# The late halves of the modulation are spread to all partitions by two fp32r passes instead of one f32 matmul

## The chip, the cores and the metric

The kernel runs on one core of a Trainium2 chip. The metric is the device time of one launch in microseconds. Its five engines work side by side and are tied only by semaphores: TensorE (PE), VectorE (DVE), ScalarE (ACT), GpSimd (POOL), and SyncE (SP), which here issues nearly all loads.

## The reference, cut to what matters

One transformer block: a norm scaled and shifted by a modulation, a mixer of three kinds of attention, and a feed-forward part that chooses experts by product keys (PEER). x is 512 tokens by 1024. The part at issue is the modulation: `c` is one vector of 1024, and its product with `w_ada` gives 6144 numbers, six rows of 1024, which are the same for each token.

```python
cs = jax.nn.silu(c)
mod = jnp.einsum('bd,de->be', cs, w_ada[l]) + b_ada[l]
sh1, sc1, g1, sh2, sc2, g2 = [m[:, None, :] for m in jnp.split(mod, N_MOD, axis=-1)]
h = rmsnorm(x, norm1_g[l]) * (1.0 + sc1) + sh1
x = x + g1 * mixer(h, w_in[l], w_out[l], lam, lam_init, subln_g[l], sinks[l])
h = rmsnorm(x, norm2_g[l]) * (1.0 + sc2) + sh2
x = x + g2 * peer_ffn(h, peer_wq[l], peer_keys[l], peer_u[l], peer_v[l])
```

## The kernel before

**The modulation.** Six rows are cut into twelve halves of 512 columns, numbered 0 to 11 in the order sc1, sh1, g1, sc2, sh2, g2 (`ADA_HALVES`). A half's weights, 1024 x 512, lie in SBUF as eight blocks of 128 x 512, one of the 1024 inputs to a partition and block. VectorE multiplies each block by its column of silu(c) and adds them up (`mod_half`, L1588; eight instructions at L1599 and L1602), which leaves 128 partial sums for each column in `mod_acc`. The sum over the partitions is TensorE's: a matmul with a 128 x 128 matrix of ones as weights (`mod_row`, L516; the matmul at L521) adds them up and writes the total to all 128 partitions of a bank of PSUM, "a row". VectorE then copies the row to its place in SBUF (`mod_row` of VectorE, L1609: L1615 or L1618). Halves 0 to 3 (sc1, sh1) are needed as columns and go another way; halves 4 to 11 are the eight late ones.

**The precision.** An f32 matmul takes the engine longer than one of the rounded format fp32r (the rows below show both). Large products in this kernel are made in fp32r: an operand is split into a rounded part (hi) and the rest (lo), and two or three fast passes are added up in PSUM. The weights of ones need no split.

**The order around it.** Each engine's program is written out by hand. The mixer runs 64 jobs, J = 0 to 63 (a tile of 128 tokens and a head; the heads of one kind have two softmax maps each): TensorE makes the scores (L611) two jobs ahead; VectorE scales and masks them (L1707, the softmax step); ScalarE takes the exponential (L1311); for that kind VectorE combines the two maps (L1723 to L1727, `combine`); TensorE transposes the result (L624) and multiplies it with the values (L644). Between them TensorE makes projections of x with w_in (L562 to L564 and L582 to L584), whose weights ScalarE rounds (L1263) and GpSimd subtracts (L1167), with loads by SyncE (L1012). The late halves are threaded through this. Half 4 is summed on VectorE before the jobs (L1676, L1679), half 5 right behind it (L1689), and their rows come between the first projections. Of halves 6 to 11 two of the eight blocks are added in each of four jobs out of five: half 6 + J//5, its last two in J = 3, 8, 13, 18, 23, 28 (L1836). The row of a half is asked for by TensorE in J = 5, 10, ... 30 (L734), behind that job's part of a projection, and copied out by VectorE in the same J (L1838), behind the softmax step, a combine if there is one, and the first two sums of the next half.

**What ties them.** `s_accd` counts summed halves. TensorE waits for it before a row; SyncE waits for it before it loads the weights of the half after next into the same place (L1002), and its other loads stand behind that in its queue. Rows and projections take turns in two banks of PSUM (G and S2), each of which must be copied out before it is filled again. The scores take turns in S0 and S1, which the softmax step frees. `done(engine, instruction, semaphore)` makes an engine wait for its own result before it goes on.

Of the kernel before, what the change touches and what calls it, by code (L numbers as in the profile page):

```python
# [6 lines left out]
P = 128  # L7
D, S = 1024, 512
KD = D // P
# [88 lines left out]
def peer_block_kernel(nc, x, c_col, norm1_col, w_ada, b_ada, w_in, w_out, lam_vecs, subln_row, sinks_row,  # L98
# [4 lines left out]
    with ctx:  # L103
        def sb(name, shape, dt=f32):
            return ctx.enter_context(nc.sbuf_tensor(name, shape, dt))

        def sem(name):
            return ctx.enter_context(nc.semaphore(name))
# [4 lines left out]
        def at(name, kib, shape, dt=f32):  # L113
            return nc.alloc_sbuf_tensor_at(name, shape, dt, offset=base + int(kib * 1024))
# [22 lines left out]
        g1_row = at("g1_row", 168, [P, D])  # L137
        g2_row = at("g2_row", 172, [P, D])
        mod_acc = at("mod_acc", 176, [P, 2, 512])
        sh_acc = at("sh_acc", 184, [P, D])  # L140
        o_tile = [at(f"o_tile{i}", kib, [P, D]) for i, kib in enumerate((140, 144, 180, 184))]
        o_sq = at("o_sq", 188, [P, NA * HD])
# [59 lines left out]
        fin_row = at("fin_row", 96, [P, D])  # L202
        ident = sb("ident", [P, P])
        ones = sb("ones", [P, P])
        dist = sb("dist", [P, S])
        dist_w = sb("dist_w", [P, 2 * P])
        q_scale = sb("q_scale", [P, len(Q_TILES)])
# [55 lines left out]
        s_inhi, s_inlo = sem("w_in_hi_ready"), sem("w_in_lo_ready")  # L263
        s_h1hi, s_h1lo = sem("h1_hi_ready"), sem("h1_lo_ready")
        s_wout_c = sem("w_out_of_c_loaded")
        s_wohi, s_wolo, s_othi = sem("w_out_hi_ready"), sem("w_out_lo_ready"), sem("o_hi_ready")
        s_wout, s_keys, s_fin = sem("w_out_loaded"), sem("keys_loaded"), sem("final_loaded")
        s_wq = [sem(f"wq_loaded{j}") for j in range(4)]
# [120 lines left out]
        ADA_HALVES = [(s, b) for s in ADA_ORDER for b in range(2)]  # L389

        ADA_PIECES = [(0, 0, 2), (0, 2, 4), (0, 4, 6), (0, 6, 8), (1, 0, 2), (1, 2, 4), (1, 4, 6), (1, 6, 7), (1, 7, 8)]
        XT_BANKS = ["S2", "S0", "S1", "T0", "T1", "O0", "O1", "S2"]

        def key_tiles(i, j):
# [61 lines left out]
        def _(pe):  # L456
# [59 lines left out]
            def mod_row(n):  # L516

                b = side["next"]
                ps = take(b, ("row", n))
                pe.wait_ge(s_accd, n + 1)  # L520
                pe.matmul(ps[:, :], ones[:, :], mod_acc[:, n % 2, :], start=True, stop=True).then_inc(full[b], 1)  # L521

            def first_two():

# [617 lines left out]
        def _(pool):  # L1142
# [2 lines left out]
            pool.memset(power[:, :], -0.5).then_inc(s_power, 1)  # L1145
            pool.memset(ident[:, :], 0.0).then_inc(s_const, 1)
            pool.memset(ones[:, :], 1.0).then_inc(s_const, 1)
            pool.iota(dist[:, :], [[-1, S]], base=S - P, channel_multiplier=1,
                      allow_small_or_imprecise_dtypes=True).then_inc(s_const, 1)
            pool.iota(iota16[:, :], [[1, TOPK]], base=0, channel_multiplier=0,  # L1150
# [419 lines left out]
        def _(dve):  # L1570
# [17 lines left out]
            def mod_half(n, first, last):  # L1588

                acc = mod_acc[:, n % 2, :]  # L1590
                w = ada_late[n % 2]
                if first == 0:
                    half_used(dve, n - 2)
                    dve.wait_ge(s_ada[n % 2], 16 * ((n - 4) // 2 + 2))
                for k in range(first, last):
                    if k == 0:

                        dve.wait_ge(s_bh[n % 3], 16 * ((n - 4) // 3 + 1))
                        ins = dve.scalar_tensor_tensor(out=acc, in0=w[:, k, :], scalar=c_silu[:, k:k + 1],  # L1599
                                                       in1=b_half[:, n % 3, :], op0=ALU.mult, op1=ALU.add)  # L1600
                    else:
                        ins = dve.scalar_tensor_tensor(out=acc, in0=w[:, k, :], scalar=c_silu[:, k:k + 1], in1=acc,  # L1602
                                                       op0=ALU.mult, op1=ALU.add)
                    if k < KD - 1:
                        done(dve, ins, s_dv)
                    else:
                        ins.then_inc(s_accd, 1)

            def mod_row(n):  # L1609
                ps = taken(dve, ("row", n))  # L1610
# [621 lines left out]
```

## Time and profile before

| | |
|---|---|
| median of 3 runs | 1568.89 us (1568.38 to 1573.02) |
| profiled execution | 1570.63 us |
| its span in the trace | 1568.8 us |
| TensorE busy | 1526.6 us (97%) |
| VectorE busy | 1338.7 us (85%) |
| ScalarE, GpSimd busy | 660.1 us (42%), 486.0 us (31%) |
| spread matmuls (L521) | first at 69.5 us, last at 170.5 us |
| mixer with its projections | to some 310 us; behind it the experts |

A busy share of TensorE says little by itself, since its matmuls overlap and their ends are modelled; the distance of two starts is the time that one takes of the engine. In a timeline a bracket behind an instruction gives how long its engine stood idle before it, and which instruction ended that. Idle time of an engine counts only where another waits for it.

### The profile page before, as it was taken

To read this page: it belongs to the slowest core of one execution; us is meant where nothing else is said; L and a number is where in the kernel's file an instruction comes from. 1 tells how busy PE (TensorE), PEld (TensorE's weight loads), DVE (VectorE), ACT (ScalarE), POOL (GpSimd) and SP (SyncE) were. 2 spreads that over 40 slices of the span, in tenths; PEclk is the share of its full clock that TensorE was granted. 3 is DMA by queue.
4 is the path that set the end of the run, shared out by engine and by line. 5 is a ranking of instruction groups with operands and counts; after the bars stand their busy time and mean duration, and the time that the engine had idled before them with its cause. 6 is when DMAs were issued, how large, how long until landed. Compare 5 with 4: busy or idle time off the path is not lost.

```text
span 1568.8 us, 24555 instructions
## 1 busy us (share of the span) xinstructions
PE 1526.6 (97%) x8259; PEld 1362.5 (87%) x8259; DVE 1338.7 (85%) x2877; ACT 660.1 (42%) x1143; POOL 486.0 (31%) x450
## 2 busy tenths in 40 slices
PE   4999999999999999999999999999999999999997
PEld 3887777888999999999999999999999998888886
DVE  6688665649999989899698898899999998999977
ACT  4444553233344756657433333333333432333232
POOL 1121300033450000020265545456566663223000
PEclk9999999999999999999999999999999999999999
DMA  9744410122355565677799999999999999999773
GB/s 367 274 166 148 148 68 1 55 95 81 114 173 173 198 215 196 239 234 265 280 397 339 342 347 340 347 337 367 375 375 377 367 344 353 378 347 351 245 244 103
DMA packets 160467, 398.77 MB, mean 254 GB/s; under 512 B 11753, under 2 KB 75369, under 8 KB 158705
## 3 DMA queue, kind: packets, MB, share of 16 engines
q1 hardware_dynamic: 112992, 227.06, 41.4%
q0 software_dynamic: 36864, 134.23, 23.2%
q10 hardware_dynamic: 10514, 36.30, 5.9%
q8 instruction: 47, 0.77, 0.2%
q14 instruction: 50, 0.41, 0.1%
HBM read 359.27 MB, written 38.27 MB: 253 GB/s over the span
## 4 chain that ended last, share of the span: by engine, by line
PE 82%; DVE 13%; DMA 1%; ACT 1%; issue 1%; ACTq 0%; DVEq 0%; SPq 0%
PE bank_S L908 16%; PE bank_T L908 11%; PE bank_O L859 6%; PE bank_O L857 6%; PE bank_O L858 6%; PE bank_T L886 5%; PE bank_G L908 5%; PE bank_S L857 3%; PE bank_S L858 3%; PE bank_S L859 3%; PE bank_O L644 2%; PE bank_S L611 2%; DVE mod_acc L1908 1%; DVE v_sb L1914 1%; DVE v_sb L1901 1%; DVE si L1920 1%
## 5 line engine op out<-in xcount | busy, mean ns | idle before, releaser
L1463 ACT ACTIVATE v_hi<-v_raw 128x1024 fp32r<-128x1024 f32 x124 | 131.8, 1063 | 331.7 <-PE bank_G L908 331.7
L1435 ACT ACTIVATE u_hi<-u_raw 128x1024 fp32r<-128x1024 f32 x128 | 135.8, 1061 | 245.8 <-PE bank_O L859 137.6
L1214 POOL COPY stage<-eidx 128x1 uint32<-128x1 uint32 (+1 forms) x128 | 73.8, 576 | 465.1 <-DVE eidx L2029 209.5
L857 PE MATMUL bank_S<-h_hi,u_hi 128*128 128x384 f32 x512 | 179.9, 351 | 1.9 <-DVE u_lo L2001 1.9
L1218 POOL DMA_INDIRECT row<-in_peer_u,stage x128 | 148.3, 1159 | 103.7 <-POOL stage L1214 103.7
L859 PE MATMUL bank_O<-h_hi,u_lo 128*128 128x384 f32 x512 | 171.9, 336 | 0.0
L857 PE MATMUL bank_O<-h_hi,u_hi 128*128 128x384 f32 x512 | 171.7, 335 | 0.0
L859 PE MATMUL bank_S<-h_hi,u_lo 128*128 128x384 f32 x512 | 171.6, 335 | 0.0
L858 PE MATMUL bank_O<-h_lo,u_hi 128*128 128x384 f32 x512 | 171.5, 335 | 0.0
L858 PE MATMUL bank_S<-h_lo,u_hi 128*128 128x384 f32 x512 | 171.5, 335 | 0.0
L2097 DVE SCALAR_TENSOR_TENSOR y<-row,wgt,y 128x1024 f32<-128x1024 f32 x128 | 166.0, 1297 | 0.0
L2107 DVE TENSOR_TENSOR v_lo<-v_raw,v_hi 128x1024 fp32r<-128x1024 f32 x124 | 152.0, 1226 | 12.4 <-ACT v_hi L1463 0.8
L2120 DVE SCALAR_TENSOR_TENSOR junk<-row,h 128x1024 f32<-128x1024 f32 x128 | 155.9, 1218 | 0.0
L1218 POOL DMA_INDIRECT row<-in_peer_v,stage x128 | 141.9, 1109 | 41.9 <-issue 30.3
L908 PE MATMUL bank_S<-v_hi,w_lo 128*128 128x512 f32 x372 | 125.4, 391 | 0.0
L908 PE MATMUL bank_S<-v_hi,w_hi 128*128 128x512 f32 x372 | 125.3, 391 | 0.0
L908 PE MATMUL bank_S<-v_lo,w_hi 128*128 128x512 f32 x372 | 125.3, 391 | 0.0
L1506 ACT ACTIVATE g_out<-bank_T 128x512 f32<-128x512 f32 x96 | 104.6, 1121 | 46.7 <-PE bank_T L886 38.8
L2056 DVE TENSOR_SCALAR hot_i<-iota_k,cols 128x128 f32<-128x128 f32 x384 | 107.1, 346 | 1.0 <-PE bank_T L886 0.2
L886 PE MATMUL bank_T<-hot_i,hot_j 128*128 128x128 f32 x768 | 101.8, 275 | 1.4 <-DVE hot_j L2058 1.3
L886 PEld LDWEIGHTS bank_T<-hot_i,hot_j 128*128 128x128 f32 x768 | 97.6, 191 | 3.8 <-issue 2.2
L857 PEld LDWEIGHTS bank_S<-h_hi,u_hi 128*128 128x128 f32 x512 | 96.6, 189 | 2.9 <-issue 2.9
(374 smaller groups left out, 3646.4 us busy)
## 6 DMA issues: line engine op xcount, KB each, us to landing
u_raw<-in_u_t SPq DMA_DIRECT2D x128, 512.0 KB, 4.6
v_raw<-in_peer_v SPq DMA_DIRECT2D x128, 512.0 KB, 6.7
gates<-g_out ACTq DMA_DIRECT2D x12, 2048.0 KB, 6.8
g_in<-gates SPq DMA_DIRECT2D x32, 768.0 KB, 10.8
ada_late<-in_w_ada SPq DMA_DIRECT2D x8, 2048.0 KB, 8.5
spill<-a_act ACTq DMA_DIRECT2D x56, 192.0 KB, 2.5
a_act<-spill SPq DMA_DIRECT2D x14, 768.0 KB, 10.5
w_raw<-in_w_in SPq DMA_DIRECT2D x20, 512.0 KB, 4.0
```

Of the source, the lines that this page charges most:

```text
L857: pe.matmul(ps[:, 0:DT], u_hi[q][:, kk], h_hi[:, GT:NT, k, :], start=(k == 0), stop=False)
L858: pe.matmul(ps[:, 0:DT], u_hi[q][:, kk], h_lo[:, GT:NT, k, :], start=False, stop=False)
L859: mm = pe.matmul(ps[:, 0:DT], u_lo[q][:, kk], h_hi[:, GT:NT, k, :], start=False, stop=(k == KD - 1))
L886: mm = pe.matmul(ps[:, tok * P:tok * P + P], hot_j[:, b % 2, tok, :], hot_i[:, b % 2, tok, :], start=True, stop=True)
L908: mm = pe.matmul(y_bank[t][half][:, :], w[:, q, tt], v[:, q, half * 512:half * 512 + 512], start=(first and n == 0), stop=False)
L1218: pool.indirect_dma_start(rows[slot][:, :], None, table[:, :], bass.IndirectOffsetOnAxis(stage[:, place:place + 1], 0))\
L1435: act.activation(u_hi[c % 2][:, :], u_raw[:, c % 2, :], ACT.Copy).then_inc(s_uhi, 1)
L1463: act.activation(v_hi_end[:, i % TAIL, :] if end else v_hi[:, c % 2, :], v_raw[c % 4][:, :], ACT.Copy)\
L2056: dve.tensor_scalar(hot_i[:, B % 2, tok, :], iota_k[:, :], cols[:, 0, n:n + 1], cols[:, 2, n:n + 1], ALU.is_equal, ALU.mult)
L2097: dve.scalar_tensor_tensor(out=y0[:, :], in0=rows[2 * place + 1][:, :], scalar=wgt[:, q], in1=y0[:, :], op0=ALU.mult, op1=ALU.add).then_in ...
L2107: dve.tensor_tensor(lo[:, q, :], v_raw[c % 4][:, :], hi[:, q, :].bitcast(f32), ALU.subtract)\
L2120: dve.scalar_tensor_tensor(out=junk[:, :], in0=rows[2 * place][:, :], scalar=1.0, in1=h2[:, 0, :], op0=ALU.mult, op1=ALU.mult, accum_out=d ...
```

## The change

In eight places the single f32 matmul with `ones` is replaced by two fp32r matmuls with `ones_r`, a second matrix of ones declared as fp32r: one over the rounded part of the partial sums (`mod_hi`), one over the rest (`mod_lo`), added up in the same bank. VectorE makes the two parts behind the last sum of a half: it waits for that sum, copies `mod_acc` to `mod_hi` with rounding, waits for the copy, and subtracts the one from the other into `mod_lo`, which is the place of `mod_acc` itself. Only then does it raise `s_accd`. `mod_hi` lies where a row's result goes later or in a row not yet in use. GpSimd fills `ones_r` once, at the start, and TensorE waits for that before each row (`s_ones`).

```diff
--- before.py
+++ after.py
@@ -137,6 +137,9 @@
         g1_row = at("g1_row", 168, [P, D])
         g2_row = at("g2_row", 172, [P, D])
         mod_acc = at("mod_acc", 176, [P, 2, 512])
+
+        mod_lo = at("mod_lo", 176, [P, 2, 512], f32r)
+        mod_hi = {s: at(f"mod_hi{s}", kib, [P, D], f32r) for s, kib in ((2, 168), (4, 172), (3, 152), (5, 172))}
         sh_acc = at("sh_acc", 184, [P, D])
         o_tile = [at(f"o_tile{i}", kib, [P, D]) for i, kib in enumerate((140, 144, 180, 184))]
         o_sq = at("o_sq", 188, [P, NA * HD])
@@ -202,6 +205,7 @@
         fin_row = at("fin_row", 96, [P, D])
         ident = sb("ident", [P, P])
         ones = sb("ones", [P, P])
+        ones_r = at("ones_r", 189, [P, P], f32r)
         dist = sb("dist", [P, S])
         dist_w = sb("dist_w", [P, 2 * P])
         q_scale = sb("q_scale", [P, len(Q_TILES)])
@@ -263,6 +267,7 @@
         s_inhi, s_inlo = sem("w_in_hi_ready"), sem("w_in_lo_ready")
         s_h1hi, s_h1lo = sem("h1_hi_ready"), sem("h1_lo_ready")
         s_wout_c = sem("w_out_of_c_loaded")
+        s_ones = sem("rounded_ones_made")
         s_wohi, s_wolo, s_othi = sem("w_out_hi_ready"), sem("w_out_lo_ready"), sem("o_hi_ready")
         s_wout, s_keys, s_fin = sem("w_out_loaded"), sem("keys_loaded"), sem("final_loaded")
         s_wq = [sem(f"wq_loaded{j}") for j in range(4)]
@@ -389,6 +394,12 @@
         ADA_HALVES = [(s, b) for s in ADA_ORDER for b in range(2)]
 
         ADA_PIECES = [(0, 0, 2), (0, 2, 4), (0, 4, 6), (0, 6, 8), (1, 0, 2), (1, 2, 4), (1, 4, 6), (1, 6, 7), (1, 7, 8)]
+
+        def hi_of(n):
+
+            s, b = ADA_HALVES[n]
+            return mod_hi[s][:, b * 512:b * 512 + 512]
+
         XT_BANKS = ["S2", "S0", "S1", "T0", "T1", "O0", "O1", "S2"]
 
         def key_tiles(i, j):
@@ -517,8 +528,10 @@
 
                 b = side["next"]
                 ps = take(b, ("row", n))
+                pe.wait_ge(s_ones, 1)
                 pe.wait_ge(s_accd, n + 1)
-                pe.matmul(ps[:, :], ones[:, :], mod_acc[:, n % 2, :], start=True, stop=True).then_inc(full[b], 1)
+                pe.matmul(ps[:, :], ones_r[:, :], hi_of(n), start=True, stop=False)
+                pe.matmul(ps[:, :], ones_r[:, :], mod_lo[:, n % 2, :], start=False, stop=True).then_inc(full[b], 1)
 
             def first_two():
 
@@ -1145,6 +1158,7 @@
             pool.memset(power[:, :], -0.5).then_inc(s_power, 1)
             pool.memset(ident[:, :], 0.0).then_inc(s_const, 1)
             pool.memset(ones[:, :], 1.0).then_inc(s_const, 1)
+            pool.memset(ones_r[:, :].bitcast(f32), 1.0).then_inc(s_ones, 1)
             pool.iota(dist[:, :], [[-1, S]], base=S - P, channel_multiplier=1,
                       allow_small_or_imprecise_dtypes=True).then_inc(s_const, 1)
             pool.iota(iota16[:, :], [[1, TOPK]], base=0, channel_multiplier=0,
@@ -1601,10 +1615,11 @@
                     else:
                         ins = dve.scalar_tensor_tensor(out=acc, in0=w[:, k, :], scalar=c_silu[:, k:k + 1], in1=acc,
                                                        op0=ALU.mult, op1=ALU.add)
-                    if k < KD - 1:
-                        done(dve, ins, s_dv)
-                    else:
-                        ins.then_inc(s_accd, 1)
+                    done(dve, ins, s_dv)
+                    if k == KD - 1:
+                        done(dve, dve.tensor_copy(hi_of(n), acc), s_dv)
+                        dve.tensor_tensor(mod_lo[:, n % 2, :], acc, hi_of(n).bitcast(f32), ALU.subtract)\
+                           .then_inc(s_accd, 1)
 
             def mod_row(n):
                 ps = taken(dve, ("row", n))
```

## Rows read from the trace of the kernel before

**Rows 1.** The page's chain that ended last: share of the span by engine.

```profile
PE 82%; DVE 13%; DMA 1%; ACT 1%; issue 1%; ACTq 0%; DVEq 0%; SPq 0%
```

**Rows 2.** Table of stretches, 80 to 120 us: busy us and instructions by engine.

```profile
80.00:120.00 40.00, 39.73 (x256) 32.15 (x255) 34.77 (x69) 18.36 (x58) 8.79 (x4) 1.00 0.50 172
```

**Rows 3.** Timeline of TensorE: start, duration, line, operation; one spread row and its successor.

```profile
104.75 1.02 PE L521 MATMUL bank_G<-mod_acc,ones 128*128 128x512 f32 x2
105.61 0.38 PE L624 MATMUL bank_T<-ident,Sb 128*128 128x128 f32 x2
```

**Rows 4.** Timeline of TensorE, two neighbouring fp32r passes of a projection.

```profile
73.30 0.39 PE L564 MATMUL bank_G<-h_hi,w_in_lo 128*128 128x512 f32 x1
73.53 0.40 PE L562 MATMUL bank_G<-h_hi,w_in_hi 128*128 128x512 f32 x1
```

**Rows 5.** Groups by line, shapes apart, VectorE: busy, mean ns, idle before.

```profile
L2086 DVE TENSOR_TENSOR w_lo<-w_f,w_hi 128x384 fp32r<-128x384 f32 x124 | 69.3, 559 | 4.3
...
L2084 DVE CAST w_hi<-w_f 128x384 fp32r<-128x384 f32 x124 | 45.3, 365 | 46.7 <-PE bank_G L908 39.7
...
L1599 DVE SCALAR_TENSOR_TENSOR mod_acc<-ada_late,c_silu,b_half 128x512 f32<-128x512 f32 x8 | 8.4, 1047 | 0.0
...
L1671 DVE TENSOR_TENSOR h_lo<-h,h_hi 128x512 fp32r<-128x512 f32 x8 | 5.2, 688 | 0.1
```

**Rows 6.** Timeline of VectorE, the first spread row copied out.

```profile
70.58 0.69 DVE L1618 COPY g_row<-bank_G 128x512 f32<-128x512 f32 x1 [2.93 <-PE bank_G L521]
```

**Rows 7.** Timeline of VectorE behind the last sums of half 11.

```profile
164.04 1.53 DVE L1602 SCALAR_TENSOR_TENSOR mod_acc<-ada_late,c_silu,mod_acc 128x512 f32<-128x512 f32 x2
165.49 0.42 DVE L1707 CUSTOM_DVE_ANT_0 Sb<-bank_S,dist 128x256 f32<-128x256 f32 x1
```

**Rows 8.** Instructions of the tile mod_acc: duration in ns, min/median/max.

```profile
L1602 DVE SCALAR_TENSOR_TENSOR mod_acc<-ada_late,c_silu,mod_acc x56: 741/752/2900, 47.7 to 164.8; 128x512 f32<-128x512 f32 x56
```

**Rows 9.** Timeline of GpSimd: its subtractions for w_in beside halves 6 and 8.

```profile
88.75 2.39 POOL L1167 TENSOR_TENSOR w_in_lo<-w_raw,w_in_hi 128x1024 fp32r<-128x1024 f32 x1 [7.52 <-ACT w_in_hi L1263]
109.31 5.17 POOL L1167 TENSOR_TENSOR w_in_lo<-w_raw,w_in_hi 128x1024 fp32r<-128x1024 f32 x2 [18.17 <-ACT w_in_hi L1263]
```

**Rows 10.** Timeline of VectorE behind half 6.

```profile
84.72 3.11 DVE L1602 SCALAR_TENSOR_TENSOR mod_acc<-ada_late,c_silu,mod_acc 128x512 f32<-128x512 f32 x4
88.00 0.48 DVE L1707 CUSTOM_DVE_ANT_0 Sb<-bank_S,dist_w,nsinks 128x256 f32<-128x256 f32 x1 [0.16 <-PE bank_S L611]
...
92.65 0.69 DVE L1615 SCALAR_TENSOR_TENSOR a_row<-bank_S,a_row 128x512 f32<-128x512 f32 x1
```

**Rows 11.** Timeline of VectorE behind half 7, and in half 8.

```profile
103.31 0.48 DVE L1707 CUSTOM_DVE_ANT_0 Sb<-bank_S,dist_w,nsinks 128x256 f32<-128x256 f32 x1 [2.68 <-PE bank_S L611]
...
110.11 6.49 DVE L1602 SCALAR_TENSOR_TENSOR mod_acc<-ada_late,c_silu,mod_acc 128x512 f32<-128x512 f32 x4
```

**Rows 12.** Timeline of TensorE, where it waited for the copy of row 8.

```profile
120.54 0.50 PE L562 MATMUL bank_S<-h_hi,w_in_hi 128*128 128x512 f32 x1 [0.60 <-DVE sh_row L1618]
```

**Rows 13.** Timeline of VectorE, first idle times behind halves 9 and 10.

```profile
130.54 0.48 DVE L1707 CUSTOM_DVE_ANT_0 Sb<-bank_S,dist_w,nsinks 128x256 f32<-128x256 f32 x1 [1.61 <-PE bank_S L611]
...
145.71 0.29 DVE L1707 CUSTOM_DVE_ANT_0 Sb<-bank_S,dist 128x128 f32<-128x128 f32 x1 [0.89 <-PE bank_S L611]
```

**Rows 14.** Timeline of TensorE behind half 11, and the same pair one job on.

```profile
165.66 0.61 PE L644 MATMUL bank_O<-v_sb,pT 128*128 128x128 f32 x4
166.41 0.91 PE L611 MATMUL bank_S<-qkT 32*128 32x384 f32 x4
...
171.18 0.61 PE L644 MATMUL bank_O<-v_sb,pT 128*128 128x128 f32 x4
171.72 0.91 PE L611 MATMUL bank_S<-qkT 32*128 32x384 f32 x4
```

**Rows 15.** Groups by line, TensorE, 0 to 560 us: transposes of x.

```profile
L487 PE MATMUL bank_S<-ident,x_sb 128*128 128x128 f32 x16 | 4.7, 432 | 13.3 <-ACT x_sb L1256 13.3
```

**Rows 16.** Waits of SyncE's queue, 0 to 330 us: total, times, longest.

```profile
SPq L1002 <- DVE mod_acc L1602: 22.6, 5, 8.2
```

## The prediction, made before the change was run

> **What bounds the kernel now.** I read the chain of work that ended last first. By engine it is 82% TensorE and 13% VectorE [rows 1], so a saving on TensorE counts, unless VectorE is what releases TensorE at that place. The spread matmuls that the change touches lie between 69 and 171 us (table of the profile), where the twelve halves of the modulation are summed and spread between projections and attention jobs. In the table of stretches, 80 to 120 us has TensorE busy 39.73 of 40 us and VectorE 34.77 of 40 [rows 2]: TensorE is nearly without gaps, VectorE has 5.2 us to spare in 40. The question is therefore where those spare microseconds lie. For that I read the timelines of both engines around each place where a half's last sum ends, looking at the bracket behind an instruction: it says how long the engine had stood idle and for whom.
>
> **Removed on TensorE.** Each of the eight late halves is spread by one f32 matmul of 128x512, which the trace records as two instructions. It starts at 104.75 and the next instruction at 105.61 [rows 3], so it holds the engine 0.86 us. In its place come two fp32r passes of the same width. Neighbouring passes of that kind start at 73.30 and 73.53 [rows 4], 0.23 us apart; two are 0.46 us. All eight are behind fp32r projection passes, so no change of kind is added ahead of them. Gain 0.40 us a half, 8 x 0.40 = 3.2 us at most.
>
> **Added on VectorE.** Behind the eighth sum of a half now come a wait of the engine for its own result, a rounding copy of 128x512 from SBUF to SBUF, a second such wait, and a subtraction.
> - Copy: no row has 512 columns. 128x384 takes 0.365 us; subtractions take 0.559 us at 384 and 0.688 at 512 [rows 5], 0.13 us for the further 128 columns. The copy at 384 is much quicker than the subtraction of that width, so it can hardly grow faster per column than that: it lies between 0.365 (no growth) and 0.69 (the subtraction, and the copy out of PSUM at 70.58 [rows 6]). I take 0.43, near the first, as that row is the same operation.
> - Subtraction: 0.69 us, the 128x512 fp32r row of h_lo [rows 5].
> - Waits: two sums with a wait between them take 1.53 us, and the next instruction, which does not wait, starts 0.08 before their end (164.04 + 1.53 = 165.57 against 165.49) [rows 7]. A sum alone is 0.75 [rows 8], so a wait costs about 0.03, and the lost overlap 0.08.
> - Sum per half: 0.11 + 0.43 + 0.03 + (0.69 - 0.08) = 1.18 us, with bounds 1.1 and 1.45. Eight halves: 9.4 us, 8.9 to 11.6.
>
> So three times as much is added to VectorE as TensorE is spared. Whether it is seen is settled place by place.
>
> **Halves 4 and 5 (before the jobs).** VectorE stood idle 2.93 us before it took the first spread row at 70.58 [rows 6]. The added 1.18 of half 5 and what half 4 pushes ahead of it, 2.4 us in all, fit under that, as TensorE's result comes only 0.4 us earlier. The projection of TensorE behind it waited for this copy, so TensorE passes on its gain. Both rows: -0.8 us.
>
> **Half 6.** Its last sums end at 84.72 + 3.11 = 87.83; the softmax step behind them had an idle 0.16 us, then GpSimd's subtraction from 88.75 to 91.14 [rows 9] held VectorE on a six-column addition, and the copy of row 6 at 92.65 had no idle before it [rows 10]. Here VectorE is the bound, so the 0.4 of row 6 is not seen. The 1.18 us would be, but VectorE stands still until 91.14 anyway for GpSimd: the work slides into that stop. I charge 0.4 us for GpSimd's start being pushed by one added subtraction (bounds 0 and 1.2). Net +0.4.
>
> **Half 7.** The softmax step behind it waited 2.68 us for TensorE [rows 11]: hidden, row 7 gains. -0.4.
>
> **Half 8.** From 110.11 four sums take 6.49 us, as two subtractions of GpSimd run from 109.31 to 114.48 [rows 9, 11]. There is no idle on VectorE from there to the copy of row 8, and TensorE waited 0.60 us for that copy at 120.54 [rows 12]. All of the 1.18 is seen and the 0.4 of row 8 is not. +1.2.
>
> **Halves 9 and 10.** VectorE's first idle times behind them are 1.61 and 0.89 us, both for TensorE [rows 13]. The first covers 1.18. The second is a little short of 1.18, but what it delays is a softmax step whose result TensorE uses two jobs later, so I take both as hidden. -0.8 (bound of the second: +0.3).
>
> **Half 11.** Its last sums end at 165.57, and the softmax step at 165.49 had no idle before it [rows 7]. That step frees the bank that TensorE's scores at 166.41 need. That those scores waited is seen by the distance from the matmuls ahead: 0.75 us there, 0.54 at the next place (171.18 to 171.72) [rows 14]. 0.2 us is already lost there, so the added 1.18 are seen nearly in full: +1.1 (bounds 0 and 1.2). Row 11 itself comes later and gains: -0.4.
>
> **Sum.** -0.8 + 0.4 - 0.4 + 1.2 - 0.8 + 1.1 - 0.4 = +0.3 us. Nothing behind 176 us is changed, and the work there hangs on TensorE's place in its queue, so I carry the shift to the end undiminished.
>
> **Edits at no cost.** One more 128x128 fill on GpSimd ahead of the constants: TensorE's transposes stood 13.3 us waiting for ScalarE's normalised x [rows 15]; without that cover it would cost 0.2 us. Two more satisfied waits on TensorE: none. The signal of a summed half comes 1.18 us later. SyncE's queue waited five times for it before a 2 MB weight load [rows 16], with the bias piece and the loads of w_in queued behind it; but the first sum of each half never waited for a load (0.0 idle, x8 [rows 5]), so the loads have room. Were it gone, a half would start 1.18 us later.
>
> **What the skill says against it.** The rows show sums with two SBUF inputs stretched while GpSimd subtracts, and softmax steps out of PSUM not. By the Trainium skill, "SBUF — State Buffer", section "SBUF: two separate sides", the pair of ports shared by VectorE and GpSimd is an exclusive lock, taken by a VectorE operation with two SBUF inputs or in a two-port mode; both added operations would be of that sort. The trace agrees for the sums.
>
> **Rivals.**
> 1. All of it is hidden. VectorE's 5.2 idle microseconds in 40 speak for it, the places of halves 8 and 11 against. -3.2: 1565.7 us.
> 2. The forecast, VectorE seen at halves 8, 11 and partly 6: +0.3.
> 3. The lock: an added operation meets a GpSimd subtraction that no sum met before, and one place loses a whole one, 2.39 us [rows 9]. 0.3 + 2.4 = +2.7: 1571.6 us. For it: GpSimd starts at moments that depend on TensorE and ScalarE, which move by up to 1 us.
> 4. VectorE is the bound throughout the jobs, so that every added microsecond is seen: +9.4 - 3.2 = +6.2, 1575.1 us, slower. It decides as soon as the idle behind halves 7, 9 and 10 is only the slack of a ring of softmax, exponential and scores that a later step also eats. The idle times of 2.68 and 1.61 speak against it.
> 5. The edit does not do what it says: the two passes together hold TensorE as long as the old one, 0.86 us. Then the gain of 3.2 is gone and the forecast is 0.3 + 6 x 0.4 = +2.7 (six gains are counted in it): 1571.6 us.
>
> **How the numbers follow.** Profiled execution: 1570.63 us, of it 1568.8 the span; the median of the runs is 1568.89. +0.3 gives 1570.9 for a profiled execution and 1569.2 against the median. Chances: forecast 0.50, rival 1 0.18, rival 3 0.15, rival 4 0.13, rival 5 0.04. The range must reach from rival 1, less about 0.5 for the spread of runs, to just under rival 4: 1565.0 to 1574.8 us. A measurement of this kernel can tell about 0.3%, 4.7 us, from no change. Only rival 4 and the lock struck twice lie beyond it: slower 0.14. Faster by as much is more than the whole gain, leaving 0.05 for what I don't see. Same: 0.81.
>
> **What would show it.** In the profile after: the spread matmuls at 0.23 us distance, 16 records of fp32r; a copy of 0.43 and a subtraction of 0.69 behind each half; TensorE's wait for the copy of row 8 grown from 0.6 to some 2.2 us; scores after half 11 about 1 us late; no new wait on a load. Compare start times of one TensorE instruction after rows 5, 7, 8, 10 and 11 in both traces: the shifts should run about -0.8, -0.8, +0.4, -0.4, +0.3. Wrong would be: a shift that keeps falling (rival 1), one that grows at every half (rival 4), or one that goes on changing behind 176 us.

## The result and the profile after

In 14 alternating runs of each, the changed kernel took 1573.83 us in the median (1572.75 to 1575.19) and the kernel before 1570.20 (1568.38 to 1573.02). The ratio is 1.0025, with a 95% interval of 1.0018 to 1.0032: 3.9 us slower, 2.8 to 5.0. The forecast was +0.3 us, 1569.2, with a range of 1565.0 to 1574.8. The two medians stand 3.6 us apart; the text goes by the ratio. The time lies inside the range and the sign held, but the change is clearly slower, and the 3.6 us between +0.3 and +3.9 were not forecast. They are what the experiments are for. The profiled execution took 1574.76 us, its span 1572.6, against 1570.63 and 1568.8.

The page of the changed kernel: busy time of the engines, and the chain that ended last [rows 1].

```profile
PE 1524.8 (97%) x8259; PEld 1363.2 (87%) x8259; DVE 1348.5 (86%) x2893; ACT 660.4 (42%) x1143; POOL 486.2 (31%) x451
...
PE 80%; DVE 15%; ACT 2%; issue 1%; DMA 1%; ACTq 0%; DVEq 0%; SPq 0%
```

TensorE is busy 1.8 us less than before, VectorE 9.8 us more (1338.7 before). That this is near the predicted 9.4 is in part chance: the sixteen new instructions took 11.1 us, 2.1 of them in one stretched copy (half 10, below), and other instructions got shorter, the sums of `mod_acc` by 2.1. The chain has moved by two points from TensorE to VectorE.

**The terms of the sum.** TensorE's and VectorE's timelines around half 6 show the new instructions (start, duration, line).

```profile
90.47 0.40 PE L533 MATMUL bank_S<-mod_hi,ones_r 128*128 128x512 f32 x1
90.71 0.40 PE L534 MATMUL bank_S<-mod_lo,ones_r 128*128 128x512 f32 x1
90.94 0.27 PE L637 MATMUL bank_T<-ident,Sb 128*128 128x128 f32 x1
```

```profile
87.55 0.43 DVE L1620 CAST mod_hi<-mod_acc 128x512 fp32r<-128x512 f32 x1
88.02 0.69 DVE L1621 TENSOR_TENSOR mod_lo<-mod_acc,mod_hi 128x512 fp32r<-128x512 f32 x1
...
92.47 0.69 DVE L1630 SCALAR_TENSOR_TENSOR a_row<-bank_S,a_row 128x512 f32<-128x512 f32 x1
```

The two passes stand 0.24 and 0.23 us apart where the f32 matmul took 0.86 [rows 3]: the gain is 0.4 us a row, as said. The copy takes 0.43 us and the subtraction 0.69, and from the end of the sums at 87.52 (84.41 + 3.11) to the next instruction at 88.62 it is 1.10, with 0.08 of lost overlap: 1.18. So the sizes were right where nothing of GpSimd's is in the way.

**Where it went.** The best measure is the start of one and the same TensorE instruction in both traces, the transposes of each job (L624 before, L637 after), less the difference that the first projections already had at 52.56 us (0.11 us here, from the loads at the start). Minus is earlier than before.

```
transposes of job     0     5     6    10    15    17    20    25    29    31   then: at 285 us
start before, us   81.3  92.0  94.9 105.6 118.5 124.1 132.8 149.5 165.5 175.4
changed kernel    -0.83 -1.22 -0.27 -0.68 -0.67 +2.10 +1.69 +2.09 +2.08 +3.32   +2.77
predicted         -0.8        -0.4  -0.8  -0.8  +0.4   0.0  -0.4  -0.4  +0.3
```

Rows 4 and 5 gave 0.83, rows 7 and 9 gave 0.41 each. Halves 6, 8, 10 and 11 each took something, and half 8 more than twice what was said. TensorE's waits, 60 to 220 us (who waited for whom: total, times, longest) name them.

```profile
PE bank_S L624 <- DVE low L1722: 3.8, 5, 1.3
PE bank_S L575 <- DVE sh_row L1633: 1.4, 1, 1.4
PE bank_S L595 <- DVE a_row L1630: 1.1, 1, 1.1
```

Before, these were 1.0, 0.6 [rows 12] and 0.2 us. The projection at L575 waits for the copy of row 8, the one at L595 for that of row 6, the scores at L624 for softmax steps, 0.34 us at row 8, 0.74 behind half 10, 1.34 and 0.35 behind half 11, and the 1.0 of before.

**Half 8.** TensorE, around row 8:

```profile
117.39 0.47 PE L533 MATMUL bank_S<-mod_hi,ones_r 128*128 128x512 f32 x1 [0.16 <-DVE mod_lo L1621]
...
119.08 0.70 PE L624 MATMUL bank_S<-qkT 64*128 64x256 f32 x4 [0.34 <-DVE low L1722]
121.17 0.66 PE L575 MATMUL bank_S<-h_hi,w_in_hi 128*128 128x512 f32 x1 [1.38 <-DVE sh_row L1633]
121.62 0.63 PE L576 MATMUL bank_S<-h_lo,w_in_hi 128*128 128x512 f32 x1
122.05 0.63 PE L577 MATMUL bank_S<-h_hi,w_in_lo 128*128 128x512 f32 x1
```

The wait grew from 0.60 to 1.38 us, and two small ones (0.16, and 0.34 before the scores) came with it. But look at the matmuls behind it: 121.17, 121.62, 122.05 are 0.43 us apart, where such passes stand 0.23 apart [rows 4]. The stretches of both kernels show why. The column behind the busy times is the granted clock as a share of full speed; the columns ahead of it are TensorE, its weight loads, VectorE, ScalarE and GpSimd. First after, then before:

```profile
120.00:122.00 2.00, 0.83 (x2) 0.70 (x3) 1.97 (x7) 1.36 (x4) 1.32 (x1) 0.84 1.02 399
122.00:124.00 2.00, 2.00 (x7) 1.47 (x6) 1.97 (x2) 0.00 (x0) 1.04 (x1) 0.50 1.05 404
124.00:126.00 2.00, 2.00 (x11) 1.81 (x10) 1.93 (x4) 0.97 (x4) 0.00 (x0) 0.81 1.00 339
...
228.00:231.00 3.00, 2.57 (x18) 1.50 (x14) 2.62 (x6) 2.45 (x6) 0.00 (x0) 1.00 0.00 0
```

```profile
122.00:124.00 2.00, 2.00 (x13) 1.74 (x12) 1.93 (x4) 0.87 (x3) 0.43 (x1) 1.00 1.06 405
...
228.00:231.00 3.00, 2.71 (x11) 1.79 (x12) 2.90 (x9) 1.78 (x8) 0.00 (x0) 0.59 0.00 0
```

From 122 to 124 us the granted clock was 0.50 (1.2 of 2.4 GHz); before, it was 1.00 there. TensorE had worked only 0.83 of the two microseconds ahead. The 2.77 us lost between jobs 15 and 17 fall into two parts at the projection behind the wait. It starts at 121.17 where it was 120.54, which is +0.5 by the measure of the table, so 1.2 us are lost up to it; the other 1.6 are lost from there to job 17, where TensorE waits for nothing and only works slowly. In the other direction, the kernel before had a fall of its own at 228 us (0.59) that the changed one has not. It gives back 0.8 us there: +3.32 behind job 31 has become +2.77 at 285 us (there are +0.3 in between).

**Half 10.** VectorE, and then GpSimd:

```profile
142.37 1.53 DVE L1616 SCALAR_TENSOR_TENSOR mod_acc<-ada_late,c_silu,mod_acc 128x512 f32<-128x512 f32 x2
143.94 2.55 DVE L1620 CAST mod_hi<-mod_acc 128x512 fp32r<-128x512 f32 x1
146.53 0.69 DVE L1621 TENSOR_TENSOR mod_lo<-mod_acc,mod_hi 128x512 fp32r<-128x512 f32 x1
```

```profile
143.81 2.39 POOL L1181 TENSOR_TENSOR w_in_lo<-w_raw,w_in_hi 128x1024 fp32r<-128x1024 f32 x1 [8.25 <-ACT w_in_hi L1277]
```

The rounding copy took 2.55 us instead of 0.43. It ended at 146.49, 0.3 us behind GpSimd's subtraction (143.81 + 2.39 = 146.20).

**Half 11.** VectorE, and TensorE's scores of the two jobs behind:

```profile
167.82 0.43 DVE L1620 CAST mod_hi<-mod_acc 128x512 fp32r<-128x512 f32 x1
168.28 0.69 DVE L1621 TENSOR_TENSOR mod_lo<-mod_acc,mod_hi 128x512 fp32r<-128x512 f32 x1
168.89 0.42 DVE L1722 CUSTOM_DVE_ANT_0 Sb<-bank_S,dist 128x256 f32<-128x256 f32 x1
```

```profile
169.81 0.91 PE L624 MATMUL bank_S<-qkT 32*128 32x384 f32 x4 [1.34 <-DVE low L1722]
...
175.13 0.92 PE L624 MATMUL bank_S<-qkT 32*128 32x384 f32 x4 [0.35 <-DVE low L1722]
```

The softmax step starts 1.10 us behind the last sum and TensorE waits 1.34 us for it, then 0.35 once more.

### The profile page after: what moved, and what is told of

Its sections match the earlier page's. It is cut to its first block, busy times and chain, and to the rows that moved or that the text cites. A ratio compares the mean times of both kernels' runs of the same rounds, so it can differ in the third digit from the quotient of the medians.

```text
span 1572.6 us, 24572 instructions
## 1 busy us (share of the span) xinstructions
PE 1524.8 (97%) x8259; PEld 1363.2 (87%) x8259; DVE 1348.5 (86%) x2893; ACT 660.4 (42%) x1143; POOL 486.2 (31%) x451
## 4 chain that ended last, share of the span: by engine, by line
PE 80%; DVE 15%; ACT 2%; issue 1%; DMA 1%; ACTq 0%; DVEq 0%; SPq 0%
PE bank_S L921 16%; PE bank_T L921 11%; PE bank_O L872 6%; PE bank_O L870 6%; PE bank_O L871 6%; PE bank_T L899 5%; PE bank_G L921 5%; PE bank_S L870 3%; PE bank_S L871 3%; PE bank_S L872 3%; DVE mod_acc L1923 1%; PE bank_O L657 1%; DVE v_sb L1916 1%; DVE v_sb L1929 1%; DVE mod_acc L1616 1%
```

## The experiments

Two theories stood against each other. A: the loss is VectorE's added work where no idle time covers it, and what follows from it: TensorE's clock and the meeting with GpSimd. B: it is something of TensorE's own passes. The table gives TensorE's place by the measure above, for all runs (us against the kernel before; the last column is the ratio of the times with its interval). The runs were made on more than one chip, each beside runs of the kernel before, so ratios are compared and not times. The run without a ratio was executed once, for its trace.

```
transposes of job        0     5     6    10    15    17    20    25    29    31 | 285 us | ratio (95%)
changed kernel       -0.83 -1.22 -0.27 -0.68 -0.67 +2.10 +1.69 +2.09 +2.08 +3.32 | +2.77  | 1.0025 (1.0018-1.0032)
VectorE's part only  -0.02 -0.01 +0.10 +0.10 +0.50 +1.30 +1.31 +1.66 +1.65 +2.88 | +2.33  | 1.0024 (1.0013-1.0034)
TensorE's part only  -0.82 -1.18 -0.78 -1.19 -1.58 -1.16 -1.55 -1.95 -1.95 -1.95 | -1.62  | 0.9984 (0.9974-0.9993)
halves 4, 5, 7, 9    -0.82 -0.81 -0.79 -1.20 -1.19 -1.22 -1.63 -1.63 -1.64 -1.58 | -2.34  | 0.9992 (0.9983-1.0001)
wait filled          -0.82 -1.20 -0.28 -0.69 -0.70 +0.81 +0.43 +0.83 +0.83 +2.07 | +1.52  | 1.0007 (0.9998-1.0017)
changed, again       -0.80 -1.17 -0.24 -0.65 -0.63 +2.12 +1.71 +2.10 +2.10 +3.33 | +2.75  | 1.0020 (1.0011-1.0030)
half 8 only          -0.02  0.00 +0.01 +0.02 +0.01 +1.17 +1.17 +1.19 +1.18 +1.19 | +1.60  | 1.0016 (1.0007-1.0025)
changed, new order   -0.80 -1.20 -1.47 -1.88 -1.88 -2.16 -2.57 -2.17 -2.17 -0.94 | -1.58  | 0.9999 (0.9990-1.0008)
one pass, new order  -1.30 -1.90 -2.17 -2.80 -3.44 -4.11 -4.73 -5.35 -5.33 -5.32 | -5.03  | 0.9971 (0.9960-0.9982)
before, new order    -0.03 -0.04 -0.32 -0.32 -0.32 -1.00 -1.02 -1.02 -1.03 -1.02 | -1.83  | 0.9994 (0.9985-1.0003)
4 to 9, new order    -0.80 -1.20 -1.47 -1.88 -1.88 -2.16 -2.57 -2.58 -2.58 -2.53 | -2.30  | 0.9983 (0.9974-0.9992)
all but 10, new or.  -0.79 -1.18 -1.46 -1.86 -1.84 -2.13 -2.55 -2.57 -2.57 -1.34 | -2.11  | -
```

### VectorE's part alone

```diff
-                pe.wait_ge(s_ones, 1)
...
-                pe.matmul(ps[:, :], ones_r[:, :], hi_of(n), start=True, stop=False)
-                pe.matmul(ps[:, :], ones_r[:, :], mod_lo[:, n % 2, :], start=False, stop=True).then_inc(full[b], 1)
+                pe.matmul(ps[:, :], ones[:, :], mod_acc[:, n % 2, :], start=True, stop=True).then_inc(full[b], 1)
...
-                        dve.tensor_tensor(mod_lo[:, n % 2, :], acc, hi_of(n).bitcast(f32), ALU.subtract)\
+                        dve.tensor_tensor(hi_of(n), acc, hi_of(n).bitcast(f32), ALU.subtract)\
```

> VectorE makes the rounded part and the rest of each late half as in the changed kernel (the rest is written over the rounded part), but TensorE spreads the unsplit sums by the old f32 matmul. Theory A (the loss comes from VectorE's added work, at halves 6, 8, 10 and 11, plus a fall of TensorE's granted clock behind the wait at half 8): the loss of the changed kernel, +3.8 us in its profile, is without the gains of rows 4, 5, 7, 9, 10 and 11, so +5 to +7 us against the kernel before. Theory B (the two passes are what costs, in themselves or by what they do to the clock): within 1 us of the kernel before.

Ratio 1.0024, +3.8 us, its interval 2.0 to 5.3: less than the +5 to +7 of theory A, clear of theory B's 1 us. The table says why it is less. VectorE's work alone costs 1.2 us at half 8 and 1.2 at half 11, but the fall of the clock is missing, half 6 costs 0.1, since GpSimd's stop hides it and TensorE has not run ahead, and half 10 costs 0.35. TensorE around row 8 in this run:

```profile
118.56 1.10 PE L532 MATMUL bank_S<-mod_acc,ones 128*128 128x512 f32 x2 [0.15 <-DVE mod_hi L1619]
...
122.33 0.50 PE L573 MATMUL bank_S<-h_hi,w_in_hi 128*128 128x512 f32 x1 [1.38 <-DVE sh_row L1631]
122.67 0.40 PE L574 MATMUL bank_S<-h_lo,w_in_hi 128*128 128x512 f32 x1
```

The same wait of 1.38 us, and the next matmul 0.34 behind it, at full speed. So a wait of this length alone does not bring the clock down. From the projection to job 17 nothing is lost here. Before it TensorE had spent 0.93 us on the f32 row and had no wait of 0.34 before the scores; that this is not what decides is seen below (half 8 alone). At half 10 it was now the subtraction that met GpSimd (143.98 to 146.79):

```profile
143.98 2.81 DVE L1619 TENSOR_TENSOR mod_hi<-mod_acc,mod_hi 128x512 fp32r<-128x512 f32 x1
```

### TensorE's part alone

```diff
-                pe.matmul(ps[:, :], ones_r[:, :], mod_lo[:, n % 2, :], start=False, stop=True).then_inc(full[b], 1)
+                pe.matmul(ps[:, :], ones_r[:, :], hi_of(n), start=False, stop=True).then_inc(full[b], 1)
...
-            pool.memset(ones_r[:, :].bitcast(f32), 1.0).then_inc(s_ones, 1)
+            pool.memset(ones_r[:, :].bitcast(f32), 0.5).then_inc(s_ones, 1)
...
-                        ins = dve.scalar_tensor_tensor(out=acc, in0=w[:, k, :], scalar=c_silu[:, k:k + 1], in1=acc,
+                        ins = dve.scalar_tensor_tensor(out=acc if k < KD - 1 else hi_of(n), in0=w[:, k, :],
+                                                       scalar=c_silu[:, k:k + 1], in1=acc,
...
-                    done(dve, ins, s_dv)
-                    if k == KD - 1:
-                        done(dve, dve.tensor_copy(hi_of(n), acc), s_dv)
-                        dve.tensor_tensor(mod_lo[:, n % 2, :], acc, hi_of(n).bitcast(f32), ALU.subtract)\
-                           .then_inc(s_accd, 1)
+                    if k < KD - 1:
+                        done(dve, ins, s_dv)
+                    else:
+                        ins.then_inc(s_accd, 1)
```

> The eighth sum of each late half is written straight in fp32r, VectorE does nothing more, and TensorE makes two fp32r passes over it, each with weights of one half. The unrounded rest is left out, so the spread rows are rounded to fp32r. Theory A: only the gain is left, 8 x 0.4 = -3.2 us if all of it is on TensorE's path, -2.4 if rows 6 and 8 stay bound by VectorE. Theory B: no gain, or slower.

Ratio 0.9984, -2.5 us: theory A, and theory B falls. The place of TensorE shows the finer thing: rows 4, 5, 7, 9 and 10 gave 0.4 each and kept it, rows 6, 8 and 11 gave it and had it taken back at once by a longer wait:

```profile
PE bank_S L624 <- DVE low L1722: 1.4, 3, 1.0
PE bank_S L575 <- DVE sh_row L1633: 1.0, 1, 1.0
...
PE bank_S L595 <- DVE a_row L1630: 0.6, 1, 0.6
```

Before, these waits were 1.0, 0.6 and 0.2 us; each has grown by 0.4. Where VectorE is the bound, a quicker TensorE only waits longer.

### Four halves split

```diff
+        SPLIT = [4, 5, 7, 9]
...
+                if n not in SPLIT:
+                    pe.wait_ge(s_accd, n + 1)
+                    pe.matmul(ps[:, :], ones[:, :], mod_acc[:, n % 2, :], start=True, stop=True).then_inc(full[b], 1)
+                    return
...
+                    if k == KD - 1 and n not in SPLIT:
+                        ins.then_inc(s_accd, 1)
+                        return
```

> Only halves 4, 5, 7 and 9 are split and spread by two passes; 6, 8, 10 and 11 go the old way. Theory A: those four have idle time of VectorE behind them that covers the split, so each gives its 0.4 us: -1.6 us against the kernel before, 1.0 at least. Rival C (a split costs wherever it stands, as VectorE's idle time is eaten again later): +1 to +2 us.

TensorE is 1.63 us ahead from job 20 on, exactly four times 0.41, and no more than 0.06 is taken back up to job 31. The time is -1.3 us (0.9992), with an interval (-2.7 to +0.2) that just holds 0; that these four are covered is shown by the trace rather than by the time. Rival C falls.

### The wait filled

```diff
+                if J == 16:
+                    for _ in range(8):
+                        pe.matmul(bank["O0"][:, 448:512], ident[:, :], ones[:, 0:64], start=True, stop=True)
```

> The changed kernel with eight small matmuls (128x64, f32, into columns of PSUM that nobody reads) ahead of TensorE's projection in job 16, where it waited 1.38 us for the copy of row 8. Theory A: TensorE is busy in that wait, the granted clock stays at 1.00 from 120 to 126 us, and about 1.6 us come back against the changed kernel: +2.2 us against the kernel before. Rival D (the clock falls for another reason, or what it costs is made up later anyway): the time is that of the changed kernel, +3.8 us, with the same fall to 0.50.

TensorE works on through the wait, and its clock stays up:

```profile
119.52 2.00 PE L742 MATMUL bank_O<-ones,ident 128*128 128x64 f32 x16
121.33 0.48 PE L575 MATMUL bank_S<-h_hi,w_in_hi 128*128 128x512 f32 x1
```

```profile
122.00:124.00 2.00, 2.00 (x14) 1.69 (x13) 1.97 (x2) 0.78 (x3) 0.87 (x1) 1.00 1.05 399
```

From job 15 to job 17 TensorE loses 1.51 us instead of 2.77, although the filling is 0.3 us longer than the wait was; so the slow stretch cost 1.3 us in this comparison, and 1.6 without that overrun. The time, 1.0007, is 2.8 us better than the changed kernel's +3.9, but only 2.0 better than the second measurement of the same file (1.0020, next run), whose interval overlaps its own; that the filling helps is shown by the trace rather than by the time. More than the 1.3 us seen in the mixer can't be put down to this edit: in its profiled execution a further 1.7 us were won between 510 and 766 us, in a stage that the edit doesn't touch (last section).

### The changed kernel again

The same file, unchanged.

> The changed kernel once more, unchanged. Theory A: VectorE's side is the same again (the copy of half 10 stretched to 2.5 us beside GpSimd, TensorE's wait of 1.4 us for the copy of row 8, scores after half 11 late by 1.3). Whether the granted clock falls to 0.50 at 122 us again says whether that fall belongs to the kernel or to the one execution. If it falls again: +3.4 us in TensorE's place behind job 31; if not, about +1.8.

It does fall again, in the same place (granted clock in the last column but two), and the copy of half 10 is stretched again:

```profile
122.00:124.00 2.00, 2.00 (x7) 1.46 (x6) 1.97 (x4) 0.00 (x0) 1.30 (x1) 0.50 1.05 404
```

```profile
144.17 2.56 DVE L1620 CAST mod_hi<-mod_acc 128x512 fp32r<-128x512 f32 x1
```

All of TensorE's places agree with the first profile within 0.05 us, +3.33 behind job 31 as said. So the fall is not the chance of one execution: both profiles of this kernel have it.

### Half 8 alone

The kernel of the four halves with `SPLIT = [8]`.

> Only half 8 is split and spread by two passes, all others go the old way. Theory A: no idle time of VectorE covers it, so TensorE is 1.2 us later from job 16 on and nowhere else, against the kernel before, plus about 1.6 us if the wait, grown from 0.6 to some 1.8 us, makes the granted clock fall. Rival (the loss at job 16 comes from the earlier rows having brought TensorE forward, so that it waits for what was never late): 0 to +0.3 us.

TensorE loses 1.16 us between jobs 15 and 17 and neither gains nor loses elsewhere before 176 us. TensorE waits as in the changed kernel, 0.33 us before the scores and then 1.39, and yet the next matmul is 0.34 us behind, at full speed, and the clock stays at 1.00:

```profile
118.38 0.70 PE L630 MATMUL bank_S<-qkT 64*128 64x256 f32 x4 [0.33 <-DVE low L1731]
120.46 0.50 PE L581 MATMUL bank_S<-h_hi,w_in_hi 128*128 128x512 f32 x1 [1.39 <-DVE sh_row L1642]
120.80 0.40 PE L582 MATMUL bank_S<-h_lo,w_in_hi 128*128 128x512 f32 x1
```

```profile
122.00:124.00 2.00, 2.00 (x13) 1.70 (x12) 1.93 (x4) 0.95 (x4) 0.35 (x1) 1.00 0.98 354
```

So 1.2 us is the price of the split itself at half 8, and the remainder of the 2.77, 1.6 us, is the clock, as the changed kernel's own timeline says. The waits are the same within 0.01 us in the kernel that falls and in this one, so their lengths do not decide whether the clock falls; what does stays open. The time is +2.5 us, with an interval of 1.1 to 3.9 that holds the +1.2. The rival, that nothing was late here, falls.

### The changed kernel in a new order

```diff
+                if J in (5, 15):
+                    mod_row(5 + J // 5)
                 if 0 <= J < 30 and J % 5 < 4:
                     mod_half(6 + J // 5, 2 * (J % 5), 2 * (J % 5) + 2)
-                if J % 5 == 0 and 5 <= J <= 30:
+                if J % 5 == 0 and 5 <= J <= 30 and J not in (5, 15):
                     mod_row(5 + J // 5)
```

> The changed kernel, with VectorE's copy of row 6 and of row 8 put ahead of the first two sums of the next half (jobs 5 and 15), instead of behind them. Theory A: the wait for these copies, 1.1 and 1.4 us, goes, and with the second the fall of the clock: TensorE is 1.0 us earlier from job 6 on and a further 1.4 to 3 us from job 16 on than in the changed kernel; about +0.5 us against the kernel before. Rival (the two sums are then late for the next softmax step, and the wait only moves there): no better than the changed kernel.

Theory A, and by more than it said. Both copies are no longer waited for; what is left of TensorE's waits is this:

```profile
PE bank_S L624 <- DVE low L1722: 3.8, 5, 1.3
PE bank_G L575 <- DVE g_row L1633: 0.8, 1, 0.8
```

TensorE is at -2.16 in job 17, where the changed kernel is at +2.10, and the time is that of the kernel before (0.9999, within 0.1%). Halves 10 and 11 are as they were: the copy of half 10 meets GpSimd in its new place too,

```profile
138.32 2.59 DVE L1620 CAST mod_hi<-mod_acc 128x512 fp32r<-128x512 f32 x1
```

which costs 0.8 less the row's 0.4, and half 11 costs 1.2.

### The kernel before in the new order

```diff
+                if J in (5, 15):
+                    mod_row(5 + J // 5)
...
-                if J % 5 == 0 and 5 <= J <= 30:
+                if J % 5 == 0 and 5 <= J <= 30 and J not in (5, 15):
```

> The kernel before (f32 spread, no split), with VectorE's copies of rows 6 and 8 ahead of the first two sums of the next half. Theory A: TensorE's waits of 0.2 and 0.6 us for these copies go, and no more: -0.8 us in TensorE's place from job 16 on. Rival (the order alone made the changed order's run 4 us quicker than the changed kernel, whatever the spread): -3 to -4 us.

TensorE gains 0.3 and 0.7 us, 1.0 in all, and no more. So 3.2 of the 4.3 us between the changed kernel and its new order are not the order's own worth: they are the split's cost at halves 6 and 8, and the clock, which the old order exposed. The time is -0.9 us (0.9994), with 0 inside the interval.

### The new order, halves 4 to 9 split

The new order with `SPLIT = [4, 5, 6, 7, 8, 9]`.

> The changed order, halves 4 to 9 split and spread by two passes, 10 and 11 the old way. Theory A: the stretched copy of half 10 and the late scores behind half 11 are gone, and with them what rows 10 and 11 gave: TensorE stays where it is at job 24 of the run with the changed order, 2.5 us ahead of the kernel before, to the end of the mixer. -2.5 us. Rival (GpSimd's subtraction or the ring of scores strikes another place instead): -1 us or less.

TensorE holds -2.57 from job 20 to job 29 and is at -2.53 in job 31. The time is -2.7 us (0.9983, interval -4.1 to -1.3): a version with the full precision of the split that beats both kernels.

### The new order, all halves but the tenth

The new order with `SPLIT = [4, 5, 6, 7, 8, 9, 11]`.

> The changed order, all halves split but the tenth. Theory A: TensorE loses nothing at job 25 (it lost 0.8 us there and gained 0.4 by the row, net +0.4), as no operation of VectorE's is there for GpSimd's subtraction to hold up; behind half 11 it is 1.2 us late again. Rival (half 11's loss is the late effect of half 10's): nothing is lost at jobs 30 and 31 either.

This kernel was executed only once, so its places count and its time does not. Between jobs 20 and 25 nothing is lost or gained (-2.55, -2.57), where the same order with half 10 split lost 0.40 net. That net is a loss of 0.8 less a gain of 0.4. Half 11 then takes 1.23 us, as everywhere else, so it is a loss of its own. TensorE's waits for softmax steps in this run and in the one before it, in this order:

```profile
PE bank_S L630 <- DVE low L1731: 3.0, 4, 1.3
```

```profile
PE bank_S L630 <- DVE low L1731: 1.3, 2, 1.0
```

The 1.7 us more are the two scores behind half 11.

### One rounded pass in the new order

VectorE's part is that of "TensorE's part alone", the order that of the new order; on TensorE, against the changed kernel:

```diff
-                pe.matmul(ps[:, :], ones_r[:, :], hi_of(n), start=True, stop=False)
-                pe.matmul(ps[:, :], ones_r[:, :], mod_lo[:, n % 2, :], start=False, stop=True).then_inc(full[b], 1)
+                pe.matmul(ps[:, :], ones_r[:, :], hi_of(n), start=True, stop=True).then_inc(full[b], 1)
```

> The eighth sum of each late half is written straight in fp32r, and TensorE makes one fp32r pass over it; the unrounded rest is left out, so the spread rows are rounded to fp32r. Copies of rows 6 and 8 ahead of the next sums, as in the run with the changed order. Theory A: no work is added on VectorE, each row gives 0.63 us of TensorE, of which the row before half 11's scores loses some to VectorE: -4 to -5.5 us against the kernel before, better than the -2.5 of the two passes over rounded sums. Rival (VectorE is the bound through the jobs, so that what TensorE saves is waited away): -2.5 us, as that run.

-4.6 us (0.9971, interval -6.3 to -2.8): the quickest of all by its median and by TensorE's place (its interval overlaps those of the -2.5 and -2.7 us above), as the rounding is done by the eighth sum itself and VectorE has nothing to add. It buys that with the precision of the modulation rows. Its rival, that all is waited away, falls.

## Why the prediction was right or wrong, step by step

- **The sizes.** Right: 0.40 a row, 0.43 for the copy, 0.69 for the subtraction, 1.18 in all. The 9.8 us more of VectorE beside the forecast 9.4 hold a stretched copy and other instructions that got shorter, so that number confirms little.
- **Halves 4, 5, 7 and 9: covered.** Right; -0.83, -0.41 and -0.41, and the run with these four alone kept all of it.
- **Half 6: +0.4.** Right in kind, +0.56 measured (from -0.83 to -0.27). GpSimd's subtraction did have to let an added one finish first (88.02 to 88.71):

```profile
88.04 2.93 POOL L1181 TENSOR_TENSOR w_in_lo<-w_raw,w_in_hi 128x1024 fp32r<-128x1024 f32 x1 [7.12 <-ACT w_in_hi L1277]
```

  It was released at 88.04, 0.7 us earlier than before, as TensorE had run ahead 0.8 us. With that wait it took 2.93 us instead of 2.39, and so ended at 90.97 against 91.14 before; VectorE's copy of row 6, and behind it TensorE, could not come much earlier either. The 0.5 us of that wait is the term that was put at 0.4.
- **Half 8: +1.2.** The mechanism and its price were right, 1.17 measured alone. The step that failed is the one behind it: "All of the 1.18 is seen and the 0.4 of row 8 is not" took a wait to cost its own length. In this kernel TensorE's granted clock fell to 0.50 behind the wait, which cost another 1.6 us. No rival held this, though the kernel's trace already had such a fall at 228 us. It is the largest error. That the fall comes here and not behind the same waits with half 8 alone could not have been worked out from the rows; that it might come could have been priced. The wait itself was forecast at 2.2 us; it was 1.38, and the smaller waits of 0.16 and 0.34 us ahead of it bring it to 1.9.
- **Half 10: "I take both as hidden".** Wrong: an added copy met GpSimd's subtraction and took 2.1 us more, of which 0.8 were seen. Rival 3 had the mechanism, with 2.39 us and a chance of 0.15; but half 10 was not named as its place. The timeline of before had what was needed: the last sums of half 10 end at 141.67 and GpSimd's subtraction starts at 142.02, so one of two operations of 1.1 us put right behind those sums was bound to stand beside it. The reading of the idle time was off as well. The 0.89 us was not the first behind half 10: ahead of it VectorE had stood idle 0.96 us for ScalarE's exponential.

```profile
142.02 2.40 POOL L1167 TENSOR_TENSOR w_in_lo<-w_raw,w_in_hi 128x1024 fp32r<-128x1024 f32 x1 [8.68 <-ACT w_in_hi L1263]
```

```profile
143.11 0.17 DVE L1723 RECIPROCAL ra<-den 128x1 f32<-128x1 f32 x1 [0.96 <-ACT Sb L1311]
```

  So there were 1.85 us of idle time in all, enough for the 1.18 as forecast, but not for the stretched copy on top. Together with the gain of row 10, +0.40 instead of -0.4.
- **Half 11: +1.1, then -0.4.** The first was right (1.2 by TensorE's place). The second was not: the scores one job on waited 0.35 us as well, and the run with TensorE's part alone gave the row's 0.4 and took it back. +1.23 instead of +0.7.
- **Sum behind job 31.** -0.83 + 0.56 - 0.41 + 1.17 + 1.6 - 0.41 + 0.40 + 1.23 = +3.3, against +0.3. The 3.0 us are the clock 1.6, half 10 0.8, half 11 0.5, half 6 0.15.
- **"Carry the shift to the end undiminished".** Only roughly, and the sign of being wrong that the prediction named, a shift that goes on changing behind 176 us, did show: the fall at 228 us that is no longer there gave back 0.8 us, and the last stages took 0.9. The second profile of the same file had only 0.1 there (+2.75 at 285 us, +2.8 at the end), so the 0.9 is of the size of what varies by itself (below).
- **Rivals.** The first (all hidden) and the fourth (VectorE the bound throughout) are refuted by the places of TensorE; the fifth by the two passes' 0.46 us.
- **The chances.** "Same", within 0.3%, at 0.81 was right by the ratio, but only just: the upper end of the interval, 1.0032, lies beyond that bound. That the time stayed inside the range is in part luck. The range was drawn from rivals 1 and 4, which are both refuted, and the largest of the 3.0 us, the clock, stood in no rival; the second largest, half 10, had its mechanism in rival 3 alone.

## What to carry to other kernels

Work moved from the bounding engine to one with idle time is free only where that idle time lies: walk through each place, and read the engine's brackets up to the next instruction that the bounding engine waits for. Where a place isn't covered, the first remedy is the order of the other engine's queue; two copies put ahead of sums that nobody awaited yet were worth 4.3 us of TensorE's place here, as much as the change had lost (by the times 4.1 us from 1.0025, or 3.3 from the second measurement, 1.0020, to 0.9999). And when a wait of the matmul engine grows, look at the granted clock behind it as well as at the wait.

## What the runs showed of the hardware

- TensorE's granted clock went to 0.50 behind a wait of 1.4 us in both profiles of the changed kernel, and stayed at 1.00 behind waits of 1.4 us in two other kernels. One of these, half 8 alone, had the small wait of 0.33 us before the scores as well, like the 0.34 of the changed kernel. With the wait filled there was no fall, in one profile. What decides was not found. One such fall cost 1.6 us here. In the kernel before, one at 228 us cost 0.8 us; eight of the twelve other profiles are without it, and those are the ones that gain 0.5 to 0.8 us between job 31 and 285 us in the table. It came or went between kernels whose places differ by less than half a microsecond: at -1.95 us (TensorE's part only) it is there, at -1.58 (halves 4, 5, 7, 9) it is not.
- The rounding copy from SBUF to SBUF, which has one input, is held up by a subtraction of GpSimd just as sums with two inputs are: 2.55 and 2.56 us in the two profiles of the changed kernel, 2.59 with the wait filled and 2.59 in the new order, each ending 0.3 us behind GpSimd's instruction. Softmax steps out of PSUM beside it kept their length (0.47 and 0.48 us inside GpSimd's subtraction from 120.05 to 122.43 in the kernel before). By the Trainium skill, "SBUF — State Buffer", section "SBUF: two separate sides", a VectorE operation in a two-port mode, or with two SBUF inputs against a GpSimd operation that reads SBUF, and that of GpSimd exclude each other for the whole instruction. The traces agree in that one waits for the other, and in both directions: the copy waited for GpSimd, and at half 6 GpSimd waited 0.5 us for the subtraction, which has two inputs. That the copy runs in a two-port mode is shown by no trace itself.
- One execution differs from another by more than 1 us in a stage that no edit touches. The clearing of y (L2065 and its like) is at the end of the stage that begins at 510 us. Before, changed kernel, changed kernel again, wait filled:

```profile
L2065 DVE MEMSET y<- x1: 912/912/912, 765.6 to 765.6; 128x1024 f32 x1
```

```profile
L2080 DVE MEMSET y<- x1: 912/912/912, 769.0 to 769.0; 128x1024 f32 x1
```

```profile
L2080 DVE MEMSET y<- x1: 912/912/912, 768.0 to 768.0; 128x1024 f32 x1
```

```profile
L2083 DVE MEMSET y<- x1: 912/912/912, 765.4 to 765.4; 128x1024 f32 x1
```

  Against the kernel before, the changed kernel was 2.9 us late at 510 us and is 3.4 late here. The same file again was 3.1 late and is 2.4 late, so the two profiles of one file part by 1.2 us in this stage. The kernel with the wait filled was 1.5 late and is 0.2 early. What does this wasn't tried and stays open, and with it how the 3.9 us of the ratio divide exactly between the mixer (2.8 in the profile) and the rest.
